# PEER with the last 64 prompt tokens gathered sparsely, and the low parts of the second half moved from GpSimd to VectorE

## The reference

```python
q = (xb @ w_q).reshape(PEER_BLOCK, PEER_HEADS, 2, PEER_HALF)      # 8 heads
s1 = einsum('thd,kd->thk', q[:, :, 0], sub_k1)                    # 128 keys each
s2 = einsum('thd,kd->thk', q[:, :, 1], sub_k2)
v1, i1 = top_k(s1, 16); v2, i2 = top_k(s2, 16)
cand = v1[..., :, None] + v2[..., None, :]                        # 16 x 16 sums
top_s, top_pos = top_k(cand, 16)                                  # 16 experts a head
gate = softmax(top_s)                                             # expert = i1 * 128 + i2
act = gelu(einsum('thkd,td->thk', expert_u[eidx], xb))
return einsum('thk,thkd->td', gate * act, expert_v[eidx])
```

## Time and profile before

| | us |
|---|---|
| median of 3 runs | 4445.22 (4438.73 to 4447.77) |
| the profiled execution's own time | 4446.63 |
| its span, first to last instruction | 4444.8 |
| PE busy | 4184.0 (94%) |
| DVE busy | 2086.2 (47%) |
| ACT busy | 1438.7 (32%) |
| POOL busy | 2022.1 (45%) |
| mean granted TensorE clock | 0.973 of full speed |
| layer 0: stage s, stage y | about 490 to 1370, 1378 to 2095 |
| layer 1: stage s, stage y | about 2826 to 3705, 3712 to 4430 |

### The profile page before, as it was taken

How to read it: one execution, slowest core, us unless ns; L and a number is a source line. 1 busy time by engine, 2 the same in 40 slices (tenths; PEclk the granted TensorE clock), 3 DMA queues, 4 the chain that set the end, 5 groups by cost and what they waited for, 6 DMA issues and landing times.

```text
span 4444.8 us, 65560 instructions
## 1 busy us (share of the span) xinstructions
PE 4184.0 (94%) x21677; PEld 3462.1 (78%) x21677; DVE 2086.2 (47%) x5320; ACT 1438.7 (32%) x1929; POOL 2022.1 (45%) x1004
## 2 busy tenths in 40 slices
PE   7899999999998999999887799999999998999998
PEld 7898887878786888887853458887878787888887
DVE  2332578888731222222556432578888731222221
ACT  2222343434432333332220332343434332333332
POOL 3333434454335666665520003334444335666664
PEclk9999999999999999999997899999999999999999
DMA  3222344645457565652134222344645457565652
GB/s 119 67 72 73 105 159 150 201 155 191 144 176 228 187 193 185 200 177 92 62 115 143 74 65 71 104 159 151 202 154 193 143 174 229 188 193 187 196 182 81
DMA packets 345166, 659.83 MB, mean 148 GB/s; under 512 B 22009, under 2 KB 186617, under 8 KB 336249
## 3 DMA queue, kind: packets, MB, share of 16 engines
q1 hardware_dynamic: 163152, 488.74, 32.3%
q10 hardware_dynamic: 176096, 149.67, 11.5%
q0 software_dynamic: 5776, 19.72, 1.6%
HBM read 520.44 MB, written 137.61 MB: 148 GB/s over the span
## 4 chain that ended last, share of the span: by engine, by line
PE 88%; DVE 4%; issue 3%; POOL 2%; ACT 2%; SPq 1%; DMA 0%; ACTq 0%; POOLq 0%; DVEq 0%
PE acc L517 61%; PE acc L504 14%; PE misc L637 5%; PE misc L842 1%; POOL w_lo L1890 1%; PE misc L784 1%; PE acc L856 1%; DVE hot_gate L1534 1%; PE misc L527 1%; PE misc L879 1%; DVE passed L1726 1%; PE misc L672 1%; PE acc L868 1%; DVE sq L1340 0%; PE misc L581 0%
## 5 line engine op out<-in xcount | busy, mean ns | idle before, releaser
L1890 POOL TENSOR_TENSOR w_lo<-raw,w_hi 128x1024 fp32r<-128x1024 f32 x620 | 1560.1, 2517 | 2245.5 <-ACT w_hi L937 2245.5
L517 PE MATMUL acc<-h_hi,w_hi 128*128 128x512 f32 x3072 | 1232.1, 401 | 25.9 <-POOL w_lo L1890 25.6
L517 PE MATMUL acc<-h_hi,w_lo 128*128 128x512 f32 x3072 | 1219.8, 397 | 0.0
L517 PE MATMUL acc<-h_lo,w_hi 128*128 128x512 f32 x3072 | 1212.6, 395 | 0.0
L937 ACT ACTIVATE w_hi<-raw 128x1024 fp32r<-128x1024 f32 x620 | 656.7, 1059 | 1311.1 <-PE acc L517 898.9
L517 PEld LDWEIGHTS acc<-h_hi,w_hi 128*128 128x128 f32 x3072 | 579.1, 189 | 164.7 <-issue 35.6
L517 PEld LDWEIGHTS acc<-h_hi,w_lo 128*128 128x128 f32 x3072 | 579.1, 188 | 139.1
L1614 DVE TENSOR_TENSOR x<-x,acc 128x512 f32<-128x512 f32 x256 | 175.9, 687 | 1087.5 <-PE acc L517 1087.5
L517 PEld LDWEIGHTS acc<-h_lo,w_hi 128*128 128x128 f32 x3072 | 580.3, 189 | 133.6
L1534 DVE TENSOR_SCALAR hot_gate<-iota,idxT,gateT 128x128 f32<-128x128 f32 x1024 | 547.5, 535 | 0.0
L1045 ACT ACTIVATE gelu<-acc 128x512 f32<-128x512 f32 x256 | 152.9, 597 | 966.2 <-PE acc L517 935.8
(11 more groups left out here) (306 smaller groups left out, 4365.0 us busy)
## 6 DMA issues: line engine op xcount, KB each, us to landing
raw<-slabs_in SPq DMA_DIRECT2D x620, 512.0 KB, 3.4
act_d<-gelu SPq DMA_DIRECT2D x256, 256.0 KB
gate_d<-gout SPq DMA_DIRECT2D x64, 1024.0 KB
abuf<-act_d ACTq DMA_DIRECT2D x32, 2048.0 KB, 10.9
gbuf<-gate_d ACTq DMA_DIRECT2D x32, 2048.0 KB, 19.1
unit<-cv_in SPq DMA_DIRECT2D x128, 128.0 KB, 2.0
unit<-ck_in SPq DMA_DIRECT2D x64, 160.0 KB, 3.2
unit<-ck_in ACTq DMA_DIRECT2D x64, 160.0 KB, 3.2
```

The costliest lines, as they stand in the source:

```text
L517: last = pe.matmul(acc[:, par, 0, :], w[:, c, :], m(c)[:, 0:TP], start=c == 0 and w is w_hi[r] and m is m_hi, stop=c == KC - 1 and w is w_ ...
L1890: pool.tensor_tensor(w_lo[r % 2][:], raw[r][:], w_hi[r % 2][:].bitcast(F32), ALU.subtract).then_inc(lo_done, 1)
```

## The change

Prompt tokens 448 to 511 leave the dense path. ND = 448 replaces 512 as the number of columns in stages s and y, in act_d, gate_d (28 chunks of 16 tokens, before 32), abuf, gbuf, y_hi and y_lo; block 3 has 8 gate steps, before 16. The accumulators use PSUM banks acc[:, 0, par], so that acc[:, 1] is free for the sparse tokens' h.

The 64 tokens are taken in four groups of 16; with 8 heads a group fills 128 partitions. SP stores their routes to route_d and reads them back by head and token (32 small loads a layer). DVE spreads h of a group (hSP), PE turns it (`group_h`), then 16 steps on DVE dot a fetched u row with it (`group_dot`), ACT applies gelu, 16 steps add v rows in PSUM (`group_value`), ACT copies the sum, PE adds up the heads (`group_y`) and DVE adds it to x. POOL issues the fetches, one a slab from slab 104 of stage s (indirect, 128 rows of 4 KB, four buffers).

DVE takes over low_part from POOL. weigh runs one part ahead. Groups 0 and 1 are both loaded 8 slabs after the last gate step; then group j+1 is loaded as group j begins. The loops over stage y are written out on PE, DVE, ACT and POOL.

```diff
+ND = 448
+NSG = (TP - ND) // TG
+NG = ND // TG
+RB = 4
 # PE: dense
-                        last = pe.matmul(acc[:, par, 0, :], w[:, c, :], m(c)[:, 0:TP],
+                        last = pe.matmul(acc[:, 0, par, 0:ND], w[:, c, :], m(c)[:, 0:ND],
 # SP: block 3 of peer_loads
+                        steps(8)
+                        sp.wait_ge(route_done, l * NDB + 4)
+                        sp.dma_start(route_d[l].rearrange("g t k h s -> (g t) k h s"),
+                                     route[P - NSG * TG:P]).then_inc(p_route_stored, 16)
+                        steps(4)
+                        sp.wait_ge(p_route_stored, 16 * (l + 1))
+                        for g in range(NSG):
+                            for h in range(PH):
+                                sp.dma_start(routeP[h * TG:(h + 1) * TG, g], route_d[l][g, :, :, h]).then_inc(
+                                    p_route_loaded, 16)
 # PE: stage y
+                for g in range(NSG):
+                    if g + 1 < NSG:
+                        group_h(g + 1)
+                    y_group(4 * g, 0)
+                    y_group(4 * g + 1, 1)
+                    group_y(g)
+                    y_group(4 * g + 2, 0)
+                    y_group(4 * g + 3, 1)
 # ACT: load_first, called when 8 slabs have followed the last gate step
                     load_group(0, 0)
+                    load_group(1, 1)
 # ACT: stage y (y_group with load_group(j + 2, par) at its start is removed)
+                for j in range(J):
+                    par = j % 2
+                    if 0 < j < J - 1:
+
+                        act.wait_ge(y_lo_done, W0 + j * GRP)
+                        load_group(j + 1, 1 - par)
+                    for c in range(GRP):
+                        n = j * GRP + c
+                        ahead(yq0 + n // 4, n % 4, last=l == LAST_L and n == NK - 1)
+                        if j + 1 < J:
...
+                            hi_part(j + 1, c, 1 - par)
 # DVE: new steps
+                dve.tensor_tensor_reduce(out=row[:].rearrange("p (k d) -> p k d", k=2), in0=acc[:, 1],
+                                         in1=row[:].rearrange("p (k d) -> p k d", k=2), scale=1.0, scalar=0.0,
+                                         op0=ALU.mult, op1=ALU.add, accum_out=dotP[:, k:k + 1]).then_inc(p_rows_used, 1)
...
+                    dve.scalar_tensor_tensor(total, row, weightP[:, k:k + 1], total, ALU.mult, ALU.add).then_inc(
+                        p_rows_used, 1)
 # DVE: stage y
+                for n in range(NK):
+                    j, c = divmod(n, GRP)
+                    if j + 1 < J:
+                        if c == 0:
+                            weigh(j + 1, 0)
+                        if c + 1 < GRP:
+                            weigh(j + 1, c + 1)
+                    if TAIL + n < NSG * 2 * TOPK:
+                        sparse(TAIL + n)
+                    if j + 1 < J:
+                        low_part(j + 1, c)
+                    if n % 32 == 18 and n // 32 < NSG:
+                        group_add(l, n // 32)
+                    dve.wait_ge(slab_done, BASE[f"y{l}"] + n + 1)
+
+                    dve.wait_ge(acc_free_dve, DVE_TILES[f"y{l}"] + n + 2 - GRP + 1)
+                    dve.tensor_tensor(x[:, c, 0:ND], x[:, c, 0:ND], acc[:, 0, c % 2, 0:ND],
+                                      ALU.add).then_inc(acc_free_dve, 1)
 # POOL: from slab 104 of s to the end of y
+                for n in range(done, 2 * NK):
+                    ahead(q0 + n // 4, n % 4, last=l == LAST_L and n == 2 * NK - 1)
...
+                    while fetched < min(n - done + 3, NSG * 2 * TOPK):
+                        group_fetch(fetched)
+                        fetched += 1
```

More of the change, by code:

```diff
@@ L147, in build @@
         sel_t = sb("sel_t", [SR, TS])
+        sel_p = sb("sel_p", [P, TG])
         ms_at = place[0]
@@ L222, in build @@
         qS = take("qS", [P, 2, SR])
+        idxT = take("idxT", [P, 2, ND])
+        gateT = take("gateT", [P, ND])
         y_tail = take.end
-        gelu = take("gelu", [P, 2, TP])
+        gelu = take("gelu", [P, 2, ND])
+        gates_at = take.end
         HG = TG // 2
@@ L228, in build @@
         gout = [take(f"gout{r}", [P, P, TG]) for r in range(2)]
-        rows_at = take.end
+        gates_end = take.end
         rows = [take(f"rows{r}", [P, D]) for r in range(2)]
@@ L233, in build @@
         v_sum = take("v_sum", [P, D])
+        h_sp = at("h_sp", [P, KC, NSG * TG], F32, take.end - 2 * 4 * D)
+        v_out = v_sum
+        routeP = take("routeP", [P, NSG, 3, TOPK])
+        expertP = take("expertP", [P, NSG, TOPK], U32)
+        dotP = take("dotP", [P, TOPK])
+        dot_actP = take("dot_actP", [P, TOPK])
+        weightP = take("weightP", [P, TOPK])
+        hSP = at("hSP", [P, KC, P], F32, ms_at)
         hS = at("hS", [P, KC, SR], F32, ms_at)
@@ L399, in build @@
         block = es.enter_context(nc.Block())
-        N_CONST = 9
+        TAIL = 2 * TOPK - 8
+        Y_FIRST = 2 * TOPK - TAIL
+        STEPS_OF = [min(P, ND - b * P) // HG for b in range(NDB)]
+        N_CONST = 10
         N_ATT = 13
@@ L687, in peer, with group_h, group_y @@
                             gates(i + (H0 + b * P // HG + r), r % 2)
-                    done[0] += P // HG
+                    done[0] += STEPS_OF[b]
+                def group_h(g):
+                    pe.wait_ge(p_hS_done, l * NSG + g + 1)
+                    if g == 0:
+                        pe.wait_ge(s_y_added, l + 1)
+                    else:
+                        pe.wait_ge(p_rows_used, (l * NSG + g - 1) * 2 * TOPK + TOPK)
+                    for c in range(KC):
+                        last = pe.transpose(acc[:, 1, c // 4, (c % 4) * P:(c % 4 + 1) * P], hSP[:, c, :], ident[:])
+                    last.then_inc(p_h_rows_done, 1)
+                def group_y(g):
+                    pe.wait_ge(p_v_out_done, l * NSG + g + 1)
+                    for c in range(KC):
+                        last = pe.matmul(misc[:, 2, c * TG:(c + 1) * TG], v_out[:, c * P:(c + 1) * P], sel_p[:],
+                                         start=True, stop=True)
+                    last.then_inc(p_y_done, 1)
+                s_only(2)
+                group_h(0)
                 s_only(NK - done[0])
@@ L1571, in peer @@
                     dve.wait_ge(slotT_done, B + 1)
-                    for r in range(w // HG):
+                    if b == 3:
+                        dve.wait_ge(s_y_done, l + 1)
+                        dve.tensor_tensor(x[:, :, TP:T], x[:, :, TP:T],
+                                          acc[:, 1, 0, 0:KC * TS].rearrange("p (c t) -> p c t", c=KC),
+                                          ALU.add).then_inc(s_y_added, 1)
+                        dve.tensor_tensor(h_sp[:], h_hi[:, :, ND:TP].bitcast(F32), h_lo[:, :, ND:TP].bitcast(F32),
+                                          ALU.add).then_inc(dve_step, step.up())
+                        dve.wait_ge(dve_step, step.at)
+                        group_rows(l, 0)
+                    for r in range(STEPS_OF[b]):
                         half = H0 + t0 // HG + r
@@ new lines, in sparse @@
+                def sparse(i):
+                    g, k = divmod(i, 2 * TOPK)
+                    if k < TOPK:
+                        group_dot(l, g, k)
+                    else:
+                        group_value(l, g, k - TOPK)
+                    if k == TOPK and g + 1 < NSG:
+                        group_rows(l, g + 1)
+                for i in range(TOPK):
+                    sparse(i)
+                for c in range(GRP):
+                    weigh(0, c)
+                for c in range(GRP):
+                    sparse(TOPK + c)
+                    low_part(0, c)
@@ L1964, in peer @@
-                yq0 = BASE[f"y{l}"] // 4
-                def y_group(j, par, last):
-                    for c in range(GRP):
-                        ahead(j * 2 + (yq0 + c // 4), c % 4, last=l == LAST_L and last and c == GRP - 1)
-                        if not last:
-                            low_part(j + 1, c, 1 - par)
-                with pool.Fori(0, J - 2, 2) as j:
-                    y_group(j, 0, False)
-                    y_group(j + 1, 1, False)
-                y_group(J - 2, 0, False)
```

209 lines of the change are left out of this document (120 added, 89 removed).

## The result

The changed kernel took 4545.39 us (median of 4 runs, 4531.90 to 4549.46), the one before 4442.85 beside it (4438.73 to 4447.77). The ratio is 1.0228, 95% interval 1.0215 to 1.024: slower, by 102.5 us where 87 were predicted. The profiled run took 4548.63 us for a span of 4546.8, 1.8 more, as before.

A forecast was written before the change was run, and what follows sets the result against it. TensorE, 88% of the span, was taken to bound the kernel. Terms -330 -28 +372 +20 +24 +12 +8 +4 +5 = +87 us took the span of 4444.8 to a forecast of 4532, range 4430 to 4625.

The forecast's parts named there:

- Fewer columns: Stages s and y: 512 slabs with matmuls of 448 columns in place of 512, -330 us (-328 to -354).
- Group loads: Stage y: later group loads leave TensorE idle 11.4 us plus 1.9 restart at 28 boundaries, +372 us (316 to 482).
- Group matmuls: TensorE: eight turned tiles and eight small matmuls for each sparse group, +20 us (10 to 30).
- Gate steps bound by DVE: Stage s, blocks 1 and 2: DVE allows 7.1 us a step, TensorE wants 6.73; 64 steps, +24 us (0 to 40).
- Block 3: Stage s: SP waits for route_done at step 8, delaying stores, gelu and w_hi; 4 us a layer, +8.
- 32 small loads on SP: Block 3: 0.34 us each to issue, 11 us against a lead of three slabs: nothing (20 if each took 1.1).
- Between the stages: From stage s to y: idle and restarts of 21.2 us a layer for 18.6 before, +5 us (-25 to +30).
- The seam: Between stages s and y: gelu, two hi_parts, low, sparse, low leave TensorE idle 3.9 us; with a restart, 5.8.
- the eight gate steps fewer a layer: Stage s: sixteen gate steps go, eight a layer, at 1.79 us each, -28 us.
- the routing pair: Routing in stage s: the w_lo pair of 8.09 us meets shorter slabs, 1.5 a block, +12 us (0 to 25).
- the h_sp prelude: Stage s: h_sp and hSP come ahead of the one-hots, 2 us a layer, +4.
- DVE has four operations a slab: Stage y, sign for the rival that helpers miss 4.88 us a slab: +0.4 for some 200 slabs, 4612 us, chance 0.18.

The follow-up runs named there:

- e1: Changed kernel with stage y's group loads issued eight slabs before use, as in the kernel before (also called the lead version): 4150.73 us, ratio 0.934 to the kernel before.
- e8: Changed kernel with v-row fetches of groups 1 to 3 moving 64 of 1024 elements a row, late loads kept: 4515.49 us.
- e5: e1 with 3 stores and 8 loads of routes on SP in place of 1 and 32: 4143.29 us, -7.4 against e1.
- e4: e1 with the load of group 1 issued after the first group's gelu, not right behind group 0's: 4118.44 us, -32.3 against e1.
- e7: e1 with the 16 value steps on DVE before the eight low parts at the end of stage s: 4127.27 us, -23.5 against e1.
- e6: Changed kernel with the edits of e1, e4, e5 and e7 together: 4087.32 us, ratio 0.9198 to the kernel before.
- e2: Kernel before with only the load time changed: group j+1 loaded as group j begins, in place of j+2: 4786.58 us, ratio 1.0771.
- e3: Changed kernel with the load of group j+2 issued at the seventh slab of group j, two slabs earlier: 4404.38 us.
- e10: Changed kernel with the load of group j+2 issued at the fifth slab of group j, four slabs earlier: 4170.60 us.
- e9: e1 with stage y's low parts back on GpSimd, except those of group 0: 4159.29 us, 8.6 more than e1.

## Why the prediction was right, and where its terms were off

The forecast (4532) lies 13 us from the median, and its mechanism is the one that the runs show: late group loads, 28 stalls of DVE for gbuf and of TensorE behind it. That it comes so near is in part luck, since errors cancel, between the terms and within the largest. By its steps:

- **Fewer columns**, -330. Measured in e1: a slab of y 5.53 to 4.85 (28 ns a matmul for 27); a slab of s 5.58 to 4.84 to 4.88, where I had 4.93. That is some -355, at the end of the range I gave; blocks 0 to 2 gained 47.7 a layer, by my terms 38.
- **Group loads**, +372 (13.3 each). Measured: 14.1 each by e1, 395. DVE's wait is 15.7 (14 to 17 was said), TensorE's idle 11.3 (11.4), clock 0.89 in stage y. The bytes' share of the engines, on which the term hung, is shown by e8. But the idle came out right by errors that cancel; counted in layer 0 from abuf's issue, at the twelve boundaries with fetches beside:
  - The landing takes 21.4, not 19.3 (some 6.8 MB pass, I had 5.97).
  - TensorE stalls 14.9 after the issue, not 12.9. The sum had the issue behind w_hi and hi_part; in the trace abuf's queue row (1410.72) stands beside that w_hi (1410.67) and ahead of the hi_part (1411.64).
  - From landing to restart are 5.5, not 5.0. Together the idle is 12.0.
  - At j = 13 and 14 the idle is 8.4 and 6.4. My own count has the last fetches at slab 103, so these two loads have none beside them; they landed in 17.6 and 17.4 after gbuf's issue, and I charged them like the rest.
  - The restart costs 15 x 0.17 = 2.6 (the row 1437.62 above and what follows it), not 1.9. This is what makes 14.1 of 13.3.
- **Group matmuls**, +20: in e1 1.69 and 0.87 a group, 10 a layer, 20.
- **Gate steps bound by DVE**: 6.99 a step in blocks 1 and 2 (7.1), but only after the first six of a block, which take 6.63 as in block 0. By this some 40 of the 64 steps are bound, for an estimate of +15, not +24. Right in kind; no run took it apart.
- **Block 3**: gelu waits for its store, behind SP's wait for route_done, 8.14 us. I had +8 in all; the trace shows the wait, no run its price.
- **32 small loads on SP**, "nothing (20 if each took 1.1)". Their row, the chain's group and one line's durations:
```profile
1104.03 21.01 SPq L486 DMA_DIRECT2D routeP<-route_d x32
...
L486 SPq DMA_DIRECT2D routeP<-route_d x64: 587/593/1522, 1104.0 to 3513.6; - x64
...
1129.97 0.55 ACT L1111 ACTIVATE gelu<-acc 128x448 f32<-128x448 f32 x1 [7.90 <-DMA act_d<-gelu]
```
  An issue takes 0.59, not the 0.34 of the earlier trace rows, 21 us with what lies between, and ScalarE waits for its store. Cost: 7 us (e5).
- **Between the stages**, +5 (-25 to +30). This step was mis-sized. The double issue was there, 15.3 us blocked for 13.9, and costs 16 a layer (e4). The seam was taken as a plain row of operations, idle 3.9 and a restart; it is the circle above, 12 a layer (e7). Against the 18.6 of before that is +9 to +10 a layer, some +20; a little more, since e6 still has TensorE idle there for 2.4 and 2.0.
- **The rest**, the eight gate steps fewer a layer (-28), the routing pair (+12) and the h_sp prelude (+4), was not separated.

So the errors cancel between the terms too: columns some 25 and gate steps some 9 better, loads 23, seam 15 to 20 and SP 7 worse.

That DVE has four operations a slab was right as a worry and harmless: the Trainium skill (SBUF — State Buffer, Who interferes with whom) has a DVE operation with two SBUF inputs and a GpSimd reader lock each other out. The trace agrees: weigh and low_part beside w_lo (1434.80 to 1437.53 and 1438.85 to 1441.23; each ends some 0.5 after it), and weigh alone:
```profile
1435.76 2.24 DVE L1727 TENSOR_TENSOR abuf<-abuf,gbuf 128x448 f32<-128x448 f32 x1
...
1439.07 2.65 DVE L1734 TENSOR_TENSOR h_lo<-abuf,h_hi 128x448 fp32r<-128x448 f32 x1
...
1442.18 0.61 DVE L1727 TENSOR_TENSOR abuf<-abuf,gbuf 128x448 f32<-128x448 f32 x1
```
The one-hot of row 800.01 has one tensor input and is not a case of this; weigh and low_part are. With such waits counted DVE is busy for 478.69 us in a stage y of 632.60, and TensorE loses nothing (e1).

## What to carry to other kernels

When work is taken from the bound engine, look first at what moves in time around it: here the cheaper slabs were worth some 355 us, and one group load issued eight slabs later took 395. A transfer's landing time is no constant; it holds for the traffic that passed beside it, and a stall that goes brings that traffic back. An engine that both issues transfers and does work in order should not issue a second large one right behind the first, and a wait that closes a circle over three engines (step, fetch, split, slab) is seen only by writing down what stands behind each wait.

## What the runs showed of the hardware

- A second group load issued right behind the first holds the issuing engine: 12.03 us for an issue that takes 0.42 at most in e4 and e6, where the two are 8 slabs apart. ScalarE at slab 112 of the lead version (queue rows, then its next operation):
```profile
1207.80 0.42 ACTq L1133 DMA_DIRECT2D abuf<-act_d  x1
1208.25 0.60 ACTq L1135 DMA_DIRECT2D gbuf<-gate_d  x1
1208.88 12.03 ACTq L1133 DMA_DIRECT2D abuf<-act_d  x1
1220.94 1.78 ACTq L1135 DMA_DIRECT2D gbuf<-gate_d  x1
1223.00 1.06 ACT L1002 ACTIVATE w_hi<-raw 128x1024 fp32r<-128x1024 f32 x1 [14.92 <-issue]
```
- The same load's gbuf landed (medians) in 18.2 us in e2 (2.10 MB, no fetches beside it), 21.1 in the changed kernel (1.84 MB, TensorE idle for part of it), and 24.3 to 26.5 in e1, e3 and e10 (1.84 MB, TensorE idle for less of it or for none).
- Loads, slabs and fetches at 304 GB/s over 528 us, a DMA share of 0.92, still left TensorE busy for 527.6 of them (e9).
